# The end of the token-mixing stage of a two-block transformer kernel, rearranged

## What is computed

```python
# dilated attention: three groups g of two heads, merged by a softmax over their log-sum-exps
s = einsum('bqhd,bqkhd->bhqk', qg, kk) * scale
p, lse = _masked_softmax(s, valid)            # lse = max + log(sum of exp)
wts = softmax(stack(lses), axis=0)
y_b = sum(wts * stack(outs), axis=0)
# merging
g_a, g_b, g_c = split(sigmoid(merge_g), 3)    # three gates, each 256 x 1024
merged = g_a * (y_a @ br_nsa) + g_b * (y_b @ br_dil) + g_c * (y_c @ br_fox)
return merged @ w_out
```

## Time and profile before

| | us |
|---|---|
| median of 3 runs (lowest, highest) | 2089.19 (2086.98, 2090.71) |
| profiled execution, its own time | 2087.08 |
| its span | 2085.3 |
| PE busy, matmuls | 1952.7 (94%) |
| DVE busy | 1376.6 (66%) |
| ACT busy | 994.6 (48%) |
| DMA, queue of the weights, share of 16 engines | 58.1% |

### The profile page before, as it was taken

The page is one execution under the profiler, slowest core; times in us unless marked ns, Lnnn a source line. Parts: engine busy times, 40 slices in busy tenths (PEclk is TensorE's granted clock), DMA queues, the critical chain, the costliest instruction groups (busy, mean ns, idle before and its releaser), DMA issues.

```text
span 2085.3 us, 29878 instructions
## 1 busy us (share of the span) xinstructions
PE 1952.7 (94%) x12658; PEld 1737.9 (83%) x12658; DVE 1376.6 (66%) x1467; ACT 994.6 (48%) x1159; POOL 83.0 (4%) x105
## 2 busy tenths in 40 slices
PE   7998869999997899999999899999999999989998
PEld 3977768888886899999877799989998998768997
DVE  4888558999996687666434587768765553365444
ACT  3344337777775333354445443344334553535432
POOL 1330000000000000000000000000001000000000
PEclk9988979999999899999999999999999999999999
DMA  8555328999995587545312477757864442124554
GB/s 354 230 217 193 148 98 331 372 347 353 359 365 220 218 305 290 217 182 206 147 72 81 162 290 295 277 208 285 300 222 142 182 182 82 61 101 170 195 182 152
DMA packets 63877, 458.42 MB, mean 220 GB/s; under 512 B 7040, under 2 KB 7296, under 8 KB 8832
## 3 DMA queue, kind: packets, MB, share of 16 engines
q1 hardware_dynamic: 63744, 456.51, 58.1%
HBM read 455.43 MB, written 1.05 MB: 219 GB/s over the span
## 4 chain that ended last, share of the span: by engine, by line
issue 79%; DVE 7%; PE 6%; DMA 3%; ACT 2%; POOL 1%; DVEq 1%; POOLq 0%; ACTq 0%; SPq 0%
DMA ada<-in_ada 2%; DVE acc L328 2%; DVE wlo L282 2%; PE PS L355 1%; PE PS L356 1%; PE PS L357 1%; ACT whi L276 1%; DMA raw<-in_stream 1%; PE PS L1196 1%; POOL Z L487 1%; DVE hlo L464 1%; ACT Z L443 0%; DVE acc L322 0%; DVE sm L1704 0%; DVE Z L459 0%
## 5 line engine op out<-in xcount | busy, mean ns | idle before, releaser
L282 DVE TENSOR_TENSOR wlo<-raw,whi 128x2048 fp32r<-128x2048 f32 x282 | 647.0, 2296 | 354.8 <-ACT whi L276 349.6
L276 ACT ACTIVATE whi<-raw 128x2048 fp32r<-128x2048 f32 x282 | 538.5, 1913 | 383.4 <-PE PS L357 344.8
L355 PE MATMUL PS<-whi,hhi 128*128 128x256 f32 (+1 forms) x1616 | 528.4, 327 | 36.5 <-DVE wlo L282 12.3
L356 PE MATMUL PS<-wlo,hhi 128*128 128x256 f32 (+1 forms) x1616 | 516.3, 320 | 0.0
L357 PE MATMUL PS<-whi,hlo 128*128 128x256 f32 (+1 forms) x1616 | 516.3, 319 | 0.0
L355 PEld LDWEIGHTS PS<-whi,hhi 128*128 128x128 f32 x1616 | 317.9, 197 | 62.8 <-issue 15.0
L357 PEld LDWEIGHTS PS<-whi,hlo 128*128 128x128 f32 x1616 | 317.3, 196 | 19.1
L356 PEld LDWEIGHTS PS<-wlo,hhi 128*128 128x128 f32 x1616 | 318.2, 197 | 17.6
L355 PE MATMUL PS<-hhi,whi 128*128 128x256 f32 x1152 | 326.6, 284 | 2.2 <-DVE mod L350 2.2
L357 PE MATMUL PS<-hhi,wlo 128*128 128x256 f32 x1152 | 326.0, 283 | 0.0
L356 PE MATMUL PS<-hlo,whi 128*128 128x256 f32 x1152 | 326.0, 283 | 0.0
(11 more groups left out here) (376 smaller groups left out, 1815.5 us busy)
## 6 DMA issues: line engine op xcount, KB each, us to landing
raw<-in_stream SPq DMA_DIRECT2D x285, 1024.0 KB, 4.9
ada<-in_ada SPq DMA_DIRECT2D x92, 1024.0 KB, 4.9
ada<-in_stream SPq DMA_DIRECT2D x48, 1024.0 KB, 5.1
raw<-in_ada SPq DMA_DIRECT2D x3, 1024.0 KB, 15.3
xs<-in_x SPq DMA_DIRECT2D x1, 1024.0 KB, 11.5
Z<-in_ada SPq DMA_DIRECT2D x1, 1024.0 KB, 19.2
Z<-in_ctx SPq DMA_DIRECT2D x1, 1024.0 KB, 11.4
masks<-in_masks SPq DMA_DIRECT2D x2, 512.0 KB, 9.6
```

Of the source, the lines that this page charges most:

```text
L276: nc.scalar.activation(whi[:, s], src, ACT.Copy).then_inc(hi_ready, 1)
L282: nc.vector.tensor_tensor(wlo[:, s], src, whi[:, s].bitcast(F32), ALU.subtract).then_inc(lo_ready, 1)
L355: nc.tensor.matmul(out_, ah, bh, start=start, stop=False, skip_group_check=check)
L356: nc.tensor.matmul(out_, ah, bl, start=False, stop=False, skip_group_check=check)
```

## The change

1. The group weights are computed from `nm2` and `den2` without a logarithm: with m the smallest negated maximum of the three groups, lw = exp(m - nm2), and the factor is lw / sum(den2 * lw). The difference is made after pass 15's maximum (`dil_weights`), its exponential by ACT ahead of pass 17's (`lse_sub`, `lse_exp`), and the rest, with the weighted sum of the dilated groups, between the maxima of passes 18 and 19 (`dil_out`). The fox heads follow in two parts (`fox_out`): heads of passes 14 and 15 after the maximum of pass 19, the other four after the passes.
2. y is turned in two's (`turn_two`): the first pair inside the passes' last round, the second after them, the third between the two halves of `gate_unit(11, ...)`. The split goes to `yb_hi`, `yb_lo`, which lie in `zr`, and no longer to `hhi`, `hlo`.
3. ACT does the roundings of the first two pairs first, then sigmoids 0 and 1, the third rounding, sigmoid 11, a `conv_hi`, and then sigmoids 2 to 10.
4. The last branch is computed in column halves: the first half's gating starts while PE does the second; gating and addition are done in pieces of 256 columns, and `mg` is turned and split pair by pair. Two `conv_lo` are moved behind that split, one `conv_hi` too. The banks of the branches are swapped.

The diff, cut:

```diff
@@ pe_layer, passes' end
+                if i == PASSES2:
+                    pe.wait_ge(*B["y2_made"].at(0, l))
+                    turn_two(xn, 0, 6)
+            pe.wait_ge(*B["y2_made"].at(1, l))
+            turn_two(xn, 2, 4)
             pe.wait_ge(*B["m_out"].at(10, l))
-            gate_unit(11, 7)
-            pe.wait_ge(*B["y2_made"].at(0, l))
-            turn(pe, B["y2_turned"], xn, 0, 6)
-            pe.wait_ge(*B["y2_lo"].at(2, l))
-            pe.wait_ge(*B["sig_done"].at(2, l))
+            gate_unit(11, 7, 0)
+            pe.wait_ge(*B["y2_made"].at(2, l))
+            turn_two(xn, 4, 5)
+            gate_unit(11, 7, 1)
+            pe.wait_ge(*B["y2_lo"].at(0, l))
...
-            for kk in range(2):
-                ins = rows_product(u, kk, hhi[:, 4 + kk], hlo[:, 4 + kk], 4, False, kk == 1)
-            ins.then_inc(unit_used, 1)
-            pe.wait_ge(*B["br_out"].at(2, l))
-            turn(pe, B["y2_turned"], mg, 0, DC)
+            rows_product(u, 0, yb_hi[:, 4], yb_lo[:, 4], 0, False, False)
+            for half in range(2):
+                for t in range(NT):
...
+                ins.then_inc(*(unit_used, 1) if half else B["dil_mm"].up)
+            for j in range(4):
+                pe.wait_ge(*B["br_out"].at(2 + j, l))
+                turn_two(mg, 2 * j, 4 + j)
@@ act_layer, pass 17
+                    if i == 17:
+                        act.wait_ge(*B["lse_sub"].at(0, l))
+                        nc.scalar.activation(lw, lw, ACT.Exp).then_inc(*B["lse_exp"].up)
@@ act_layer, behind the passes
-            nc.scalar.activation(lnd, den2[:, 16:28], ACT.Ln).then_inc(*B["den_ln"].up)
-            act.wait_ge(*B["lse_sub"].at(0, l))
-            nc.scalar.activation(lw, lw, ACT.Exp).then_inc(*B["lse_exp"].up)
+            split_hi(0, 6, yb_hi[:, 0:2])
+            split_hi(1, 4, yb_hi[:, 2:4])
+            for f in range(2):
+                nc.scalar.activation(G[f], G[f], ACT.Sigmoid)
+            split_hi(2, 5, yb_hi[:, 4:6])
...
-            for u in range(3):
+            for u in range(2):
                 conv_hi(act, BR0 + u + RING, E0)
-            split_act(act, B["y2_turned"], B["y2_hi"], 3, 4, l)
+            for j in range(4):
+                split_hi(3 + j, 4 + j, hhi[:, 2 * j:2 * j + 2])
+            conv_hi(act, BR0 + 2 + RING, E0)
@@ dve_layer
+                if i == 15:
+                    dil_weights()
+                if i == 18:
+                    dil_out()
+                if i == 19:
+                    fox_out(14, 2, 4, 256)
+            fox_out(16, 4, 5, 0)
...
+            for j in range(4):
+                split_lo(3 + j, 4 + j, hhi[:, 2 * j:2 * j + 2], hlo[:, 2 * j:2 * j + 2])
+            for u in range(1, 3):
+                conv_lo(dve, BR0 + u + RING, E0)
```

More of the change, by code:

```diff
@@ L1857, in pe_layer, with turn_two @@
             pe.wait_ge(*B["tb_act"].at(7, l))
+            def turn_two(src, c0, bank):
+                for c in range(2):
+                    for t in range(NT):
+                        o = c * 256 + t * P
+                        ins = nc.tensor.transpose(PS[:, bank, o:o + P], src[:, t, (c0 + c) * P:(c0 + c + 1) * P], ident)
+                ins.then_inc(*B["y2_turned"].up)
             gate_unit(0, 4)
@@ L1965, in pe_layer @@
+            pe.wait_ge(*B["m_out"].at(11, l))
             u = unit(pe, BR0 + 1, E0)
[L1966 removed]
+            rows_product(u, 0, yb_hi[:, 2], yb_lo[:, 2], 4, True, True).then_inc(*B["dil_mm"].up)
             pe.wait_ge(*B["br_out"].at(0, l))
[L1968 removed]
+            rows_product(u, 1, yb_hi[:, 3], yb_lo[:, 3], 0, True, False).then_inc(unit_used, 1)
@@ new lines, in dil_out @@
+            def dil_out():
+                dve.wait_ge(*B["lse_exp"].at(0, l))
+                nc.vector.tensor_tensor(f12, den2[:, 16:28], lw, ALU.mult)
+                dve.drain()
+                nc.vector.tensor_reduce(lsm, f12.rearrange("p (g x) -> p x g", g=3), AX.X, ALU.add)
+                dve.drain()
+                nc.vector.reciprocal(lsm, lsm)
+                dve.drain()
+                nc.vector.tensor_tensor(groups(f12), groups(lw), mid(lsm, [P, 3, 4]), ALU.mult)
+                dve.drain()
+                dve.wait_ge(*B["pv2"].at(13, l))
+                dp = dil_part
+                for g in range(3):
+                    bank, o = (6, 256 * g) if g < 2 else (4, 0)
+                    nc.vector.tensor_tensor(dp[g].rearrange("p (x n) -> p x n", x=4),
+                                            PS[:, bank, o:o + 256].rearrange("p (x n) -> p x n", x=4),
+                                            bc(f12[:, 4 * g:4 * g + 4], [P, 4, 64]), ALU.mult)
+                dve.drain()
+                nc.vector.tensor_tensor(dp[0], dp[0], dp[1], ALU.add)
+                dve.drain()
+                nc.vector.tensor_tensor(y_slot(256, 2), dp[0].rearrange("p (h t n) -> p h t n", h=2, t=2),
+                                        dp[2].rearrange("p (h t n) -> p h t n", h=2, t=2), ALU.add).then_inc(*B["y2_made"].up)
@@ new lines, in dve_layer @@
+            dve.wait_ge(unit_used, E0 * 3 + (BR0 + 1))
+            for j in range(4):
+                ins = gated(0, j, 0, mg)
+            ins.then_inc(*B["br_out"].up)
+            conv_lo(dve, BR0 + RING, E0)
+            dve.wait_ge(*B["sig_done"].at(1, l))
+            dve.wait_ge(*B["dil_mm"].at(0, l))
+            for j in range(4):
+                gated(1, j, 4, mt2[0])
+            dve.drain()
+            nc.vector.tensor_tensor(mg, mg, mt2[0], ALU.add).then_inc(*B["br_out"].up)
+            dve.wait_ge(*B["sig_done"].at(2, l))
@@ new lines, in dve_layer, with merged @@
+            dve.wait_ge(*B["dil_mm"].at(1, l))
+            def merged(j):
+                c = slice(256 * j, 256 * j + 256)
+                nc.vector.tensor_tensor(mg[:, :, c], mg[:, :, c], mt2[1][:, :, c], ALU.add).then_inc(*B["br_out"].up)
+            for j in range(2):
+                for t in range(NT):
+                    c = slice(256 * j, 256 * j + 256)
+                    nc.vector.tensor_tensor(mt2[1][:, t, c], PS[:, 2 * t, c], G[8 + j][:, t], ALU.mult)
+            dve.drain()
@@ L2330, in dve_layer @@
+            merged(0)
+            dve.wait_ge(unit_used, E0 * 3 + (BR0 + 3))
+            gated(2, 2, 0, mt2[1])
+            merged(1)
+            gated(2, 3, 0, mt2[1])
+            dve.drain()
+            merged(2)
+            merged(3)
+            for j in range(4):
+                split_lo(3 + j, 4 + j, hhi[:, 2 * j:2 * j + 2], hlo[:, 2 * j:2 * j + 2])
+            for u in range(1, 3):
+                conv_lo(dve, BR0 + u + RING, E0)
             conv_lo(dve, WO0 + RING, E0)
```

111 lines of the change are left out of this document (45 added, 66 removed).

## The result

| | before | changed |
|---|---|---|
| median, us (lowest, highest) | 2087.96 (2086.98, 2090.71), 5 runs | 2078.34 (2075.59, 2078.91), 5 runs |
| profiled execution, its own time | 2087.08 | 2078.91 |
| its span | 2085.3 | 2077.1 |

The ratio is 0.995, with an interval of 0.9937 to 0.9963: 9.6 us faster against the 5 runs of before that shared the comparison. Part of that is the base: the forecast started from the 2089.19 of three runs of before, and the five runs give 2087.96. As a difference, 5.2 us were forecast and 9.6 measured. The direction was right, the size was not.

The account below looks back on a forecast made before the run. It took PE's waits for DVE's chain in the stages behind the last filled pass as the bound, the clock second. Front -1.3, chain -5.9, clock +2.0 gave -5.2 us against 2089.19: 2084.0, range 2079.5 to 2088.5.

Parts of the forecast that it names:

- front to first branch product: Passes' end to first branch product: delayed maximum of pass 19 eats the saved wait; -0.2 us layer 0, +0.5 layer 1.
- branch products to first gating: Branch products up to first gating: layer 0's low stretch of 3.4 us has no idle ahead of it; -1.6 us.
- chain, both layers: DVE from first gating to `out_product`: 18.6 us against 21.55, -5.9 us for two layers.
- Part 4: Clock at `out_product`: PE idles again, 4 us low in layer 0 and 3.4 in layer 1; +2.0 us, bounds -1.4 and +5.0.
- the fourth rival: More is gained: `out_product` finds the clock high in both layers; -8.6 us, 2080.6; chance 0.07.
- the clock stays low longer: Rival: gate 11's first half runs low and `out_product` has more low time; 4 us lost, 2088.0; chance 0.22.
- the chain is not shortened: Rival: DVE's conversion wait doubles and pairs hold DVE, about 1.5 us a layer go; 2087.0; chance 0.10.
- the slower one: Rival: clock low through gate 11 and 3.4 us into the branches, both layers; +5.4 us, 2094.6; chance 0.05.
- What I costed at nothing: Conversions moved behind the splits and later loads on SP's queue, expected in time: no cost; otherwise at most 2.3 us each.

Follow-up runs that it names:

- the new tail alone: The changed kernel with the front of before (logarithm, group weights, turning of y, sigmoids), keeping the new last branch, pairs and moved conversions: 2081.55 us, ratio 0.997.
- the sigmoids' kernel: The changed kernel with the conversion of the unit behind the first branch put ahead of the last branch's three sigmoids on ACT: 2075.23 us, ratio 0.9931.
- the kernel with the later sum: The changed kernel with the dilated groups' weighted sum behind pass 19's maximum and y's first pair turned behind the passes: 2073.91 us, ratio 0.9935.
- the combined one: The changed kernel with gate 11 in the passes, later sum, reordered sigmoids, two y pairs turned earlier, DVE's conversion behind the second addition: 2066.79 us, ratio 0.9903.
- the turning in one piece: The changed kernel, but PE turns mg only when all four pieces are added, sixteen transposes in a row: 2083.23 us, ratio 0.9981.
- the conversion put back: The changed kernel with one 2.2 us conversion again between the second and third branch on DVE, the other behind the last addition: 2090.24 us, ratio 1.0012.
- The front with the old tail: The changed kernel with its front, but last branch and addition whole, mg turned in one go and conversions between the branches: 2087.98 us, ratio 1.0001.

## Why the prediction was wrong in size

Term by term, against the cut of the stages, where the new exponential lies ahead of the first cut. It lasts 0.21 us, as forecast, but delays pass 18 by only 0.1 us a layer:

| term | forecast | measured |
|---|---|---|
| front to first branch product, layers 0 and 1 | -0.2, +0.5 | -0.6, -0.3 (-0.66 and -0.37, and 0.1 each) |
| branch products to first gating, layers 0 and 1 | -1.6, 0 | -1.64, -0.03 |
| chain, both layers | -5.9 | -6.8 |
| clock at `out_product`, both layers | +2.0 | -1.4 |
| sum | -5.2 | -10.8 |

**The step that failed** is Part 4. It took PE's new idle for as harmful as the old one, and forecast 4 and 3.4 us of low clock at `out_product`. It was 0 and 0, the bound at the lower end, which the fourth rival had with a chance of 0.07. This one term is 3.4 of the 5.6 us by which the sum is off. The other rows are 0.9 us in the chain and 1.2 in front of it.

What the runs show in its place is the number for this kernel, and no rule. In two profiles of the changed kernel, and in one of the new tail alone, `out_product` was at 1.00 in both layers, and adding zeros to the changed kernel brought nothing. But pairs between idles as short brought low clock to `out_product` in one layer of the sigmoids' kernel, in one of the kernel with the later sum and in both of the combined one; and the turning in one piece, with an idle of 4.75 us, had 1.00 there in both layers. So it isn't shown that the pairs are what keeps the clock up, and that the forecast's low clock missed the changed kernel may be in part luck. Between ends as far apart as -1.4 and +5.0 I chose a middle that no row had; the earlier trace rows had both outcomes.

**The chain** was forecast at 18.6 us and is 18.14. The mechanism was right (conversions out of the chain, pairs, a wait), two sizes were off: the wait is 0.89 us, not 1.25, since the conversion began 1.45 us behind the gating's start (1136.96 and 1135.51), not 1.6, and took 1.9 us, not 2.0; and the last pair is turned at the high clock. That the chain is what brings most is shown by the new tail alone (5.8 us), by the turning in one piece (+5.3 us of chain, 4.9 us of time) and by the conversion put back (+5.2 us of chain).

**The front** went as described: pass 19's maximum 3 us later (3.58 between the starts, 0.6 before), an idle of 1.73 us (forecast 1.8), 10.2 us of low clock, no idle and no low clock at the branches. It was some 0.4 and 0.8 us shorter than forecast: PE took the pair's transposes and the value matmuls, from 1117.79 to 1122.39, in 4.6 us, not 5.1. Up to the first branch product costs and savings nearly cancel, as forecast. The front with the old tail measured 1.0001, but that holds 1.7 us of longer chain in the two layers as well, so it does not weigh the front alone.

**The rivals.** That the clock stays low longer did not come: gate 11 saw high clock from 1124.9, 2.5 us after its start. That the chain is not shortened, and the slower one, fell with the rows above; but the conversion put back is slower than before by 2.5 us, so the mechanism of a loss was near, at `out_product` and not in the branches. What I costed at nothing stayed hidden: `out_product` ran for 13.9 us without a stop, with the conversions behind the splits. Whether the loads issued later have a part in the 0.7 us between the stages is open.

The remaining difference is outside the stage. The sum of -10.8 and the 9.6 us between the medians differ by less than the spread of either kernel's runs (3.7 and 3.3 us).

What stays open: the parts do not add up. New tail (5.8 us) and new front (-0.6) make 5.2, together they make 9.6. In the profiles the clock explains part of it (10.3 and 3.3 us low in layer 1 of the new tail's run, 9.3 and 4.3 in layer 0 of the new front's), but one profile of each does not tell how often that happens. Nor is it shown why the program ahead of the stage shifts by up to 4 us between executions. Between the two stages the shift goes with the clock: with the front of before it is 636.5 us with 10.2 us of low clock and 637.8 to 637.9 with 13.7, and with the new front 638.5 to 638.7 with 13.7 and 640.1 with 17.1.

## What to carry to other kernels

Where an engine's idle time is waiting for a chain on another, hand over in pieces as they are ready: the pieces shorten the chain, here by 2.6 and 2.7 us. Do not count on them to keep the clock up; a low clock cost the next large product up to 2.8 us here, and the same pieces had it in some layers and not in others. Cost a step ahead of a maximum (or anything that an exponential and PE wait for) at its full duration, and move what is not asked for behind it: 2.6 us a layer here. Where an idle can't be removed, filling it with matmuls of zeros is cheap, but look first at whether the clock is low behind it at all: 3.3 and 2.8 us were gained where it was, nothing where it was not.
